# Forgetting attention in a two-block kernel: scores and value products as three fp32r passes over hi and lo parts in place of fp32 products

## The reference

```python
q = heads(q) * (HEAD_DIM ** -0.5)
log_f = jax.nn.log_sigmoid((f_logit + b_f).astype(jnp.float32))
c = jnp.cumsum(log_f, axis=1).transpose(0, 2, 1)
# for each block i of 128 queries:
s = jnp.einsum('bhqd,bhkd->bhqk', qi, k).astype(jnp.float32)
s = s + ci[..., None] - c[:, :, None, :]
s = jnp.where(k_pos[None, :] <= q_pos[:, None], s, -jnp.inf)
p = jax.nn.softmax(s, axis=-1).astype(v.dtype)
out = jnp.einsum('bhqk,bhkd->bhqd', p, v)
```

## Time and profile before

| | us |
|---|---|
| median of 3 runs | 1616.16 |
| the profiled execution's own time | 1615.99 |
| its span in the trace | 1614.2 |
| TensorE busy | 1584.2 (98%) |
| VectorE, ScalarE, GpSimd busy | 725.1, 540.3, 501.9 |
| first fp32 score product to first one-column product | 157.91 to 295.33 |

### The profile page before, as it was taken

How to read it: one execution, slowest core, us unless ns; L and a number is a source line. 1 busy time by engine, 2 the same in 40 slices (tenths; PEclk the granted TensorE clock), 3 DMA queues, 4 the chain that set the end, 5 groups by cost and what they waited for, 6 DMA issues and landing times.

```text
span 1614.2 us, 20113 instructions
## 1 busy us (share of the span) xinstructions
PE 1584.2 (98%) x7738; PEld 1310.8 (81%) x7738; DVE 725.1 (45%) x954; ACT 540.3 (33%) x801; POOL 501.9 (31%) x449
## 2 busy tenths in 40 slices
PE   7999999999999999999999999999999999999998
PEld 7877888888888888888887677888888888888886
DVE  4332665447553333323265658744445433333224
ACT  4323333223442222222254455222225422223121
POOL 2870001310188058187111600583002870000000
PEclk9999999999999999999999999999999999999999
DMA  6533122222455345344230220443322553332331
GB/s 198 162 126 104 53 77 56 79 78 78 140 147 156 104 124 156 110 143 157 79 115 30 68 64 27 132 138 122 104 85 75 154 151 83 104 111 77 109 107 52
DMA packets 189296, 170.90 MB, mean 106 GB/s; under 512 B 20656, under 2 KB 161968, under 8 KB 189232
## 3 DMA queue, kind: packets, MB, share of 16 engines
q1 hardware_dynamic: 181168, 144.84, 29.6%
q0 software_dynamic: 8064, 25.20, 5.0%
HBM read 167.91 MB, written 2.10 MB: 105 GB/s over the span
## 4 chain that ended last, share of the span: by engine, by line
PE 92%; DVE 4%; ACT 2%; POOL 1%; issue 1%; DMA 0%; DVEq 0%; SPq 0%; ACTq 0%
PE bank L1726 28%; PE bank L1727 28%; PE bank L1728 28%; PE bank L1953 1%; PE bank L1936 1%; PE bank L2005 1%; PE bank L2029 1%; PE bank L1852 1%; DVE w_lo L1175 1%; POOL inv_rms L688 1%; PE bank L1945 1%; DVE decay L1578 1%; PE bank L1893 0%; PE bank L1973 0%; PE bank L2015 0%
## 5 line engine op out<-in xcount | busy, mean ns | idle before, releaser
L1726 PE MATMUL bank<-h_hi,w_hi 128*128 128x512 f32 (+1 forms) x1504 | 566.9, 377 | 4.0 <-DVE h_lo L1203 1.6
L1727 PE MATMUL bank<-h_lo,w_hi 128*128 128x512 f32 (+1 forms) x1504 | 559.4, 372 | 0.0
L1728 PE MATMUL bank<-h_hi,w_lo 128*128 128x512 f32 (+1 forms) x1504 | 559.4, 372 | 0.0
L1175 DVE TENSOR_TENSOR w_lo<-raw,w_hi 128x2048 fp32r<-128x2048 f32 (+1 forms) x146 | 302.9, 2076 | 315.6 <-ACT w_hi L820 315.4
L1726 PEld LDWEIGHTS bank<-h_hi,w_hi 128*128 128x128 f32 x1504 | 284.4, 189 | 67.5 <-issue 14.1
L1728 PEld LDWEIGHTS bank<-h_hi,w_lo 128*128 128x128 f32 x1504 | 284.2, 189 | 49.5
L1727 PEld LDWEIGHTS bank<-h_lo,w_hi 128*128 128x128 f32 x1504 | 284.6, 189 | 45.9
L820 ACT CAST w_hi<-raw 128x2048 fp32r<-128x2048 f32 (+1 forms) x145 | 243.9, 1682 | 217.6 <-PE bank L1728 217.6
L744 POOL TENSOR_SCALAR mod_raw<-mod_raw,c_silu 128x512 f32<-128x512 f32 x96 | 169.4, 1765 | 36.2 <-DMA mod_raw<-in_mod_w 32.3
L747 POOL TENSOR_TENSOR mod_acc<-mod_acc,mod_raw 128x512 f32<-128x512 f32 x96 | 150.2, 1564 | 8.2
L1726 PE MATMUL bank<-w_hi,act_hi 128*128 128x512 f32 x352 | 137.7, 391 | 0.0
(11 more groups left out here) (353 smaller groups left out, 1754.9 us busy)
## 6 DMA issues: line engine op xcount, KB each, us to landing
raw<-in_w_in SPq DMA_DIRECT2D x102, 512.0 KB, 4.5
mod_raw<-in_mod_w POOLq DMA_DIRECT2D x96, 256.0 KB, 3.2
raw<-in_w_ffn_in SPq DMA_DIRECT2D x44, 512.0 KB, 4.8
raw<-in_w_gate SPq DMA_DIRECT2D x22, 512.0 KB, 4.0
raw<-in_w_up SPq DMA_DIRECT2D x22, 512.0 KB, 5.3
raw<-in_w_down SPq DMA_DIRECT2D x20, 512.0 KB, 4.2
raw<-in_w_ffn_out SPq DMA_DIRECT2D x20, 512.0 KB, 4.2
raw<-in_w_out SPq DMA_DIRECT2D x8, 512.0 KB, 4.1
```

Of the source, the lines that this page charges most:

```text
L1175: ins = dve.tensor_tensor(w_lo[s][:, cols], raw[s][:, cols], w_hi[s][:, cols].bitcast(F32), ALU.subtract)
L1726: pe.matmul(o, st_hi, mv_hi, start=first, stop=False)
L1727: pe.matmul(o, st_hi, mv_lo, start=False, stop=False)
L1728: return pe.matmul(o, st_lo, mv_hi, start=False, stop=last)
```

## The change

The attention's two products become three passes each.

- ScalarE makes hi parts: per head of q and k (`qk_hi_parts`, two copies of 512 columns, for head h+1 in the task i = 2 of head h), per head of v (`v_hi_part`, one copy of 512, in the task i = 3), and per task of the transposed probabilities out of bank 6 (`pt_hi_part`, 128 to 512 columns, behind the exponential of the next task and ahead of that task's other work).
- VectorE makes lo parts: per head `qk_lo_parts` (two subtractions of 512 columns, in i = 3, at the end of the task) and `v_lo_part` (one of 512, in i = 0), and per task the subtraction out of bank 6 in place of the copy.
- TensorE runs `three_passes` for scores and for each of the value products. Ahead of a head's first score product it waits for `qk_lo_done`, ahead of a head's first value product for `v_lo_done`.
- q_lo, k_lo and v_lo lie in the places of q_t, k_t and v_att. v_hi takes the place of `b_sp`, whose load moves from the small loads to SyncE's queue behind the loads of the `n_vs` units, with a wait for the last head; VectorE waits for it ahead of L1418.

```diff
 # ScalarE
+            qk_hi_parts(0)
+            for t in range(NT):
+                wait_emptied(act, n_va + 3, t)
+            v_hi_part(0)
             for s, (h, i) in enumerate(ATT_TASKS):
                 n, w = n_g + h, P * (i + 1)
                 act.wait_ge(max_ready, s + 1)
                 act.activation(prob[:, s % 2, 0:w], prob[:, s % 2, 0:w], ACT.Exp, bias=neg_max[:, s % 2:s % 2 + 1],
                                accum_out=row_sum[:, s % 2:s % 2 + 1]).then_inc(prob_ready, 1)
+                if s > 0:
+                    pt_hi_part(s - 1)
...
                 if i == 2:
                     take(n, 0, gates[:, 2 * h, :], STILL, ACT.Tanh, 0.5)
+                    if h + 1 < HEADS:
+                        qk_hi_parts(h + 1)
+                if i == 3 and h + 1 < HEADS:
+                    wait(act, pv_done, NT * h)
+                    v_hi_part(h + 1)
+            pt_hi_part(len(ATT_TASKS) - 1)
 # VectorE
+            def qk_lo_parts(h):
+
+                dve.wait_ge(qk_hi_done, h + 1)
+                for lo, t, hi in ((q_lo, q_t, q_hi), (k_lo, k_t, k_hi)):
+                    ins = dve.tensor_tensor(lo[:, h, :], t[:, h, :], hi[:, h % 2, :].bitcast(F32), ALU.subtract)
+                ins.then_inc(qk_lo_done, 1)
...
-                    dve.wait_ge(pt_ready, s)
+                    dve.wait_ge(pt_hi_done, s)
                     wait(dve, pv_done, s - 2)
-                    dve.tensor_copy(prob_t[:, b, 0:w], bank[:, 6, 0:w]).then_inc(pt_copied, 1)
+                    dve.tensor_tensor(pt_lo[:, b, 0:w], bank[:, 6, 0:w], pt_hi[:, b, 0:w].bitcast(F32), ALU.subtract).then_inc(pt_lo_done, 1)
+                if s < len(ATT_TASKS) and i == 0 and h > 0:
+                    v_lo_part(h)
+                if s < len(ATT_TASKS) and i == 3 and h + 1 < HEADS:
+                    qk_lo_parts(h + 1)
                 if s < len(ATT_TASKS) and i in (1, 2):
                     split(n_g + h + 1, part=i - 1)
 # TensorE
-                    pe.matmul(bank[:, b, 0:w], q_t[:, h, P * i:P * i + P], k_t[:, h, 0:w], start=True, stop=True)
+                    if i == 0:
+                        pe.wait_ge(qk_lo_done, h + 1)
+                    three_passes(bank[:, b, 0:w], q_hi[:, h % 2, P * i:P * i + P], q_lo[:, h, P * i:P * i + P],
+                                 k_hi[:, h % 2, 0:w], k_lo[:, h, 0:w], True, True)
...
                     for j in range(i + 1):
-                        ins = pe.matmul(bank[:, 7, P * i:P * i + P], v_att[:, j, P * h:P * h + P],
-                                        prob_t[:, b, P * j:P * j + P], start=(j == 0), stop=(j == i))
+                        js = slice(P * j, P * j + P)
+                        ins = three_passes(bank[:, 7, P * i:P * i + P], v_hi[:, h % 2, j, :], v_lo[:, j, P * h:P * h + P],
+                                           pt_hi[:, b, js], pt_lo[:, b, js], j == 0, j == i)
 # SyncE
+            sp.wait_ge(head_out, HEADS)
+            sp.dma_start(b_sp[:], a["b_spatial"][0].partition_broadcast(P)).then_inc(b_sp_in, 16)
```

More of the change, by code:

```diff
@@ L157, in build @@
         v_att = at("v_att", 80, [P, NT, D])
+        v_lo = at("v_lo", 80, [P, NT, D], F32R)
         mrg_hi = at("mrg_hi", 80, [P, KD, TOK], F32R)
@@ L172, in build @@
         k_t = at("k_t", A + 16, [P, HEADS, TOK])
+        q_lo = at("q_lo", A + 0, [P, HEADS, TOK], F32R)
+        k_lo = at("k_lo", A + 16, [P, HEADS, TOK], F32R)
+        k_hi = at("k_hi", A + 72, [P, 2, TOK], F32R)
+        q_hi = at("q_hi", A + 80, [P, 2, TOK], F32R)
+        v_hi = at("v_hi", A + 84, [P, 2, NT, P], F32R)
         v_sgu = at("v_sgu", A + 16, [P, NT, D])
@@ L177, in build @@
         prob = at("prob", A + 64, [P, 2, TOK])
-        prob_t = at("prob_t", A + 68, [P, 2, TOK])
+        pt_hi = at("pt_hi", A + 68, [P, 2, TOK], F32R)
         c_rows = at("c_rows", A + 72, [P, TOK], F32R)
@@ L253, in build @@
         states = [None] + [at(f"state_{c}", M + 9.5 + 2 * (c - 2), [P, 256]) for c in (2, 3)]
+        pt_lo = at("pt_lo", M + 16.5, [P, 2, TOK], F32R)
         row_a = at("row_a", M + 16.5, [HEADS, TOK])
@@ L342, in build @@
         c_spread, c_kept = sems("c_spread", "c_kept")
-        pt_ready, pt_copied, pv_done, head_out, gated_b = sems("pt_ready", "pt_copied", "pv_done", "head_out", "gated_b")
+        pt_ready, pt_hi_done, pt_lo_done, pv_done, head_out, gated_b = sems(
+            "pt_ready", "pt_hi_done", "pt_lo_done", "pv_done", "head_out", "gated_b")
+        qk_hi_done, qk_lo_done, v_hi_done, v_lo_done, b_sp_in = sems("qk_hi_done", "qk_lo_done", "v_hi_done", "v_lo_done", "b_sp_in")
         wsp_tr, wsp_done, v_normed, sgu_ready = sems("wsp_tr", "wsp_done", "v_normed", "sgu_ready")
@@ L501, in build @@
         POST_UNIT = [n_out + 3, n_dn + 11, n_out2 + 3, n_dn2 + 11]
-        SMALL, SMALL_2 = 10, 14
+        SMALL, SMALL_2 = 9, 14
         wf_hi, wf_lo = ktiles(wf_both, KD, 40)[:, :, 0:8], ktiles(wf_both, KD, 40)[:, :, 32:40]
@@ L579, in load_small @@
                     (gain_row[:], a["mix_post_g"][0].partition_broadcast(P)),
-                    (b_sp[:], a["b_spatial"][0].partition_broadcast(P)),
                     (sgu_g[:], column("sgu_norm_g")), (gain_2[:], column("ffn_pre_g")),
@@ L981, in _, with qk_hi_parts, v_hi_part, pt_hi_part @@
                     take(n_va + 1, t, v_att[:, t, 512 * c:512 * c + 512], chunk_pace(c))
+            def qk_hi_parts(h):
+                act.copy(q_hi[:, h % 2, :], q_t[:, h, :])
+                act.copy(k_hi[:, h % 2, :], k_t[:, h, :]).then_inc(qk_hi_done, 1)
+            def v_hi_part(h):
+                act.copy(v_hi[:, h % 2, :, :], v_att[:, :, P * h:P * h + P]).then_inc(v_hi_done, 1)
+            def pt_hi_part(s):
+                w, b = P * (ATT_TASKS[s][1] + 1), s % 2
+                act.wait_ge(pt_ready, s + 1)
+                wait(act, pv_done, s - 1)
+                act.copy(pt_hi[:, b, 0:w], bank[:, 6, 0:w]).then_inc(pt_hi_done, 1)
+            qk_hi_parts(0)
+            for t in range(NT):
+                wait_emptied(act, n_va + 3, t)
+            v_hi_part(0)
             for s, (h, i) in enumerate(ATT_TASKS):
@@ L1369, in _, with v_lo_part @@
             chunks(n_va, None)
+            def qk_lo_parts(h):
[3 more added lines that the diff above has]
+                ins.then_inc(qk_lo_done, 1)
+            def v_lo_part(h):
+                dve.wait_ge(v_hi_done, h + 1)
+                dve.tensor_tensor(v_lo[:, :, P * h:P * h + P], v_att[:, :, P * h:P * h + P], v_hi[:, h % 2, :, :].bitcast(F32),
+                                  ALU.subtract).then_inc(v_lo_done, 1)
+            qk_lo_parts(0)
+            v_lo_part(0)
             for s in range(len(ATT_TASKS) + 3):
@@ L1410, in _ @@
             dve.wait_ge(gated_b, KD)
+            dve.wait_ge(b_sp_in, 16)
             for f in range(KD):
@@ L1942, in _ @@
                     pe.wait_ge(prob_scaled, s)
-                    wait(pe, pt_copied, s - 1)
+                    wait(pe, pt_lo_done, s - 1)
                     for j in range(i + 1):
@@ L1948, in _ @@
                     (h, i), b = ATT_TASKS[s - 2], (s - 2) % 2
-                    pe.wait_ge(pt_copied, s - 1)
+                    pe.wait_ge(pt_lo_done, s - 1)
                     if i == 0:
                         wait(pe, head_out, h)
+                        pe.wait_ge(v_lo_done, h + 1)
                     for j in range(i + 1):
-                        ins = pe.matmul(bank[:, 7, P * i:P * i + P], v_att[:, j, P * h:P * h + P],
-                                        prob_t[:, b, P * j:P * j + P], start=(j == 0), stop=(j == i))
+                        js = slice(P * j, P * j + P)
+                        ins = three_passes(bank[:, 7, P * i:P * i + P], v_hi[:, h % 2, j, :], v_lo[:, j, P * h:P * h + P],
+                                           pt_hi[:, b, js], pt_lo[:, b, js], j == 0, j == i)
                     ins.then_inc(pv_done, 1)
```

## The result

| | before | changed |
|---|---|---|
| median, us | 1616.10 (4 runs) | 1650.36 (1649.62 to 1651.48, 4 runs) |
| profiled execution, us | 1615.99 | 1651.48 |
| its span | 1614.2 | 1649.8 |
| attention, first score product to first one-column product | 157.91 to 295.33 | 160.42 to 327.42 |

The account below looks back on a forecast made before the run. TensorE, 92% of the span, was taken as the bound; start 2.2, head 0 2.7, heads 1 to 6 17.2 and end 2.1 sum to 24.2 us, forecasting 1640.3. Own range 1634 to 1646, with the clock rival 1634 to 1651.

Parts of the forecast that it names:

- the rival with the falling clock: At each change of head TensorE's idle time halves the clock: 1.4 us seven times, 10 us, giving 1650; chance 0.10.
- The passes: TensorE's score and value products in three passes: +0.82 us a head, +6.6 us over eight heads.
- The narrow pass: A TensorE pass of 128 columns, held by its weight load: 0.11 us.
- the values' share: Value products on TensorE: 10 products of three passes, 3.30 us a head, 1.08 more than before.
- The scores' gain: Score products on TensorE in three passes: 1.90 us a head, 0.26 less than before.
- The sentence on the fast weight load: Skill page: fast load needs 128 weights and non-FP32 input; if fp32r qualified, narrow passes would take half of 0.11 us.
- The change of head: TensorE waits for VectorE's q_lo and k_lo before the next head's scores: 2.05 us stall, +2.87 a head, 17.2 over heads 1 to 6.
- VectorE's chain: VectorE's steps through one head, timed from its first score product, ending with q_lo and k_lo at 19.75 us.
- Start and end: First score product delayed by head 0's q and k parts, +2.2 us; head 7 and the attention's end, +2.1 us.
- Head 0: First head, with no head before it: 15.0 us before, VectorE's chain ending at 17.7, +2.7 us.
- `b_sp`: Its 512 KB load, moved later on SyncE's queue, costs nothing, as VectorE reads it only in the merge.
- second rival: Narrow TensorE passes cost 0.055 us, 264 in all, 14.5 us less: about 1626; chance 0.06.

Follow-up runs that it names:

- e5: On top of e1, ScalarE makes head 0's q_hi and k_hi ahead of its last value copies: 1625.78 us, ratio 1.0059 against the kernel before.
- e4: Changed kernel with the score products as in the kernel before, only value products in three passes: 1629.33 us, ratio 1.0076 against the kernel before.
- e10: e4 with the third value pass (v_lo by the hi part of the probabilities) left out: 1622.16 us, ratio 1.0029 against the kernel before.
- e6: e5 with the value products as in the kernel before, so only scores in three passes: 1617.47 us, ratio 0.9999 against the kernel before.
- e1: Changed kernel with VectorE making the next head's q_lo and k_lo right behind the maximum in i = 3: 1628.97 us, 21 us under the changed kernel.
- e12: Kernel before, with products nobody reads in TensorE's three waits at the end of the attention: 1615.81 us, ratio 0.9994 against the kernel before.
- e7: e5 with the third pass of the value products left out, 80 passes fewer: 1626.93 us, ratio 1.0058 against the kernel before.
- e3: Changed kernel with fp32 value products as before; scores in three passes with their wait: 1642.81 us, ratio 1.0169 against the kernel before.
- e8: e5 with value products for two query blocks at a time, passes of 256 columns: 1640.01 us, ratio 1.0129 against the kernel before.
- e2: Changed kernel with products nobody reads ahead of TensorE's wait for q_lo and k_lo at each head: 1644.04 us, 6.3 us under the changed kernel.
- e11: e8 with q, k and weight-unit parts made earlier and the attention's end waits filled with unread products: 1616.17 us, ratio 0.9992 against the kernel before.

## Why the prediction was right or wrong

- **Direction and range**: slower, as forecast, and inside the range, but at its upper end: 1650.4 against 1640.3. It lies outside the forecast's own range of 1634 to 1646; only the rival with the falling clock reaches it. That this rival named 1650 is in part luck: it had seven falls at 1.4 us, one at each change of head, and there were three at 1.6 to 1.7, one more behind the first product, and 3.4 us more of the clock's cost came behind the attention, where the rival had none.
- **The passes**: right. +0.82 us a head was forecast, and e5's heads of 17.88 are 0.94 over 16.94; the values' share, 1.08, is 1.13 in e4. The narrow pass is 0.10 to 0.11 (e10). The scores' gain was mis-sized: 0.26 a head forecast, 0.19 measured next to the value passes (e4 less e5) and 0.09 alone (e6). The sentence on the fast weight load was rightly set against the earlier trace rows. The Trainium skill, page "TensorE: Matmul & The Clock Gate", section "LDWEIGHTS (loading the stationary operand)", gives a load's time in ns as its columns divided by 1.2, an estimate of 107 ns for 128 columns. The trace agrees, with 0.11 us between loads.
- **The change of head**: right, and the largest term. 2.05 us of stall forecast, 2.04 measured (19.92 less 17.88); VectorE's chain forecast at 5.65, 15.1, 18.0, 18.5 and 19.75, measured 5.7, 15.1, 18.0, 18.5 and 19.8. e1 shows that it is this wait: without it 21 us are gone, and 25 in e5, which takes the wait at the start away too.
- **Start and end**: 2.2 and 2.1 forecast, 2.5 and 2.3 measured. Head 0, without its low clock, became 2.8 us longer; 2.7 was forecast.
- **`b_sp`**: hidden, as forecast. Its load was issued at 337.4 and landed 5.2 us later, and VectorE first read it at 389.1.
- **The clock**: here the step failed. I read from one row, a wait of 1.8 us in block two with a full clock behind it, that waits of 2 us leave the clock alone, and gave the contrary one chance in ten. In the changed kernel it fell behind the start and behind three of seven changes of head, two of them behind waits that don't differ by more than a few hundredths from those behind which it stayed; and it cost at two more places that the change doesn't touch. One row of a wait that left the clock up says that it can stay up, not that it will: in e12 it fell behind this very wait (1.76 us there, 1.77 in the kernel before). The price of one fall, 1.4 us forecast, is 1.6 to 1.7. Of the 35.5 us some 10 are the clock, 25.5 the rest, against 24.2 forecast for the rest.
- **What I didn't see**: that VectorE's list, idle for a third of a head, is nevertheless a limit 0.25 us under TensorE's (e7). The prediction had followed that list and found it 0.2 us late in the changed kernel, but it priced its second rival, the cheaper narrow pass, by TensorE's passes alone: 14.5 us less. With 80 passes left out, e7's heads came down by 0.24 us only and then waited for VectorE, so most of those 14.5 us would not have come.

## What to carry to other kernels

Three fp32r passes win over an fp32 product only where the moving side is wide enough to hide the weight load: at 128 columns they cost half again as much (0.33 us against 0.22), at 256 and more about a fifth less, so count the products by width before replacing them. Parts that are made for the next stage belong into a gap of the helper engine's list well before the stage, since a chain TensorE, ScalarE, VectorE, TensorE without work of TensorE's own in between is paid in full at each stage; and a list that is busy two thirds of the time can be the bound all the same. Where TensorE has to stand for 1.5 to 2.6 us, reckon with the low clock behind some of the waits (three of seven in the changed kernel, two of seven in e3, four of seven in e8), or fill the wait with products that nobody reads.

## What the runs showed of the hardware that I had not expected

- The same wait of 1.87 to 1.91 us was followed by the low clock behind two changes of head and by the full clock behind four others in one execution, waits of 1.52 to 1.53 us were enough for it in e8, and executions of one kernel lay up to 8.6 us apart (e3) with the mean clock 0.988 to 0.994.
- Products that write a bank nobody reads kept the clock at 2.4 GHz in all heads (e2) and behind the attention (e11, e12), although 16 one-column products follow the filled waits there.
- A low-clock stretch costs 1.6 to 1.7 us in a head, and one can be twice as long: behind the attention, around the one-column products and transposes, it lasted from 327.8 to 334.6 in the changed kernel and from 297.8 to 301.2 before.
